# Turning h before its norm is known, and bringing the norm in late

## The chip, the cores and the metric

The kernel runs on one core of one Trainium2 chip. The metric is the device time of one execution in microseconds. Three runs of the kernel before took 1638.55, 1638.58 and 1638.84 us, median 1638.58.

## The reference, cut to what matters

One residual block over 512 tokens of width 1024. Its last third is the part that the change touches:

```
h   = h + merged @ w_out                       # 512 x 1024
hn  = h * rsqrt(mean(h*h) + 1e-6) * g_ffn      # one factor per token, one per channel
qry = hn @ w_peer_q                            # 1024 -> 2048: 8 heads x 2 halves x 128
s1, s2 = qry halves @ keys                     # 128 keys each
v1, i1 = top16(s1);  v2, i2 = top16(s2)
best   = top16 of the 16 x 16 sums v1 + v2     # per head and token
gates  = softmax(best)
out    = h + sum over 16384 experts of gate * gelu(u . hn) * v
```

The top lists do not change when all scores of a token are multiplied by one positive number. The softmax and the products `u . hn` do.

## The kernel before, in words

All products of full width run on TensorE in pieces that give nearly f32 accuracy. An operand is split into a high part (f32 rounded to TensorE's fp32r) and a low part (what is left), and three matmuls are made for each pair of blocks: high x high, high x low and low x high (`PARTS`). The weights come in 512 KB items, one after the other, through four raw buffers. For each item ScalarE makes the high part (`high_w`, line 1196) and GpSimd the low part (`low_ws`, line 435; VectorE takes a few, line 1515), into two buffers that alternate. An item of a projection is 24 matmuls of 128x512 on TensorE.

The order of the work on each engine is written out by hand: each engine has one instruction stream (blocks `@block.tensor`, `.scalar`, `.vector`, `.gpsimd`, `.sync`), and the streams meet at counting semaphores. SyncE issues all DMAs in its own order.

The stretch that the change touches runs like this:

- The output projection (items 77 to 84, lines 700 and 976) fills PSUM banks 0 to 3 with the left half of h, then banks 4 to 7 with the right half. VectorE adds x (`add_x`, line 1812), and ScalarE sums the squares (`square_h`, line 1373) and takes roots (line 1388).
- VectorE takes the reciprocals and multiplies h by them (`norm_h`, lines 1818 and 1821, result `h_scaled`). TensorE turns the 32 blocks of it (`turn_block`, line 656), 16 in each half of the width.
- ScalarE reads the turned blocks out of PSUM times g_ffn into the high part of `hT_r` (line 1396); VectorE makes the low part (line 1845) and then `x_two`, which is low x 128 + high (line 1851).
- The query projection has 16 items, number 85 to 100. The first (`first_item`, lines 670, 674, 678) goes along with the arriving blocks of `hT_r`, the others are plain (`t_item`, line 687). After item 1, and from then on after every second one, TensorE makes key scores (`key_scores`, line 1023, order in `SCORES_AFTER`), two groups each time, 16 groups in all. ScalarE copies the query out (`query`, line 1412), makes the high part of the item after the next, and then copies the scores out (`score_copy`, line 1401). There are two score buffers: the copy of group g waits until VectorE has finished the lists of group g - 2 (`at_least(act, score_used, g - 1)`).
- VectorE makes the top-16 lists of a group (`first_lists` and `top16`, lines 1862 to 1872).
- The up stage multiplies 128 tiles of u with the normed h (`up`, line 1061, 16 matmuls a tile): the first of the two operands is the high part of `hT_r`, the second is `x_two`. ScalarE makes the high part of each tile (`high_u`, line 1407), GpSimd the low part of the first 56 (line 474). ScalarE's stream at the join of the two stages is: query 15, copy of scores 14, `high_u(1)`, copy of scores 15, `high_u(2)`, then gelu 0 (line 1426) and so on.
- During the first 56 tiles VectorE makes the candidate sums, the second lists and the gates (lines 1884 to 1927), and TensorE turns each of four results between tiles 20, 33, 45, 52 and the next (`turn_lists`, line 656).

Of the kernel before, what the change touches and what calls it, by code (L numbers as in the profile page):

```python
# [24 lines left out]
F32 = mybir.dt.float32  # L25
# [3 lines left out]
ALU = mybir.AluOpType  # L29
# [3 lines left out]
P = 128  # L33
T = 512
# [71 lines left out]
SCORES_AFTER = {1: (0,), 3: (1, 2), 5: (3, 4), 7: (5, 6), 9: (7, 8), 11: (9, 10), 13: (11, 12), 14: (13,), 15: (14,)}  # L106
EXP_AFTER, TURN_AFTER = (10, 20, 31, 44), (20, 33, 45, 52)
# [12 lines left out]
def build(nc, A, out, gates_dram, pre_dram, acts_dram):  # L120
    ctx = ExitStack()
    with ctx:
# [34 lines left out]
        def carve_r(name, at, size):  # L157

            return carve(name, at, size, F32R)
# [45 lines left out]
        hT_r = carve_r("hT_r", 4096, 8192)  # L205
        x_two = carve_r("x_two", 34816, 4096)
        h_scaled = carve("h_scaled", 22528, 4096)
        junk = carve("junk", 43008, 1024)
# [34 lines left out]
        hs3 = h_scaled.rearrange("p (t d) -> p t d", d=D)  # L243
# [78 lines left out]
        def block_bank(k):  # L322
# [5 lines left out]
        max_out, max_in, if_in, f_row = sem("max_out"), sem("max_in"), sem("if_in"), sem("f_row")  # L328
# [7 lines left out]
        act_step, dve_step, pool_step = sem("act_step"), sem("dve_step"), sem("pool_step")  # L336
# [3 lines left out]
        h_half, h_biased = sem("h_half"), sem("h_biased")  # L340
# [7 lines left out]
        q_scaled, conv_done, silu_done, sig_o = sem("q_scaled"), sem("conv_done"), sem("silu_done"), sem("sig_o")  # L348
# [14 lines left out]
        h_rooted, h_normed, hT_done, hT_hi, hT_out = (  # L363
            sem("h_rooted"), sem("h_normed"), sem("hT_done"), sem("hT_hi"), sem("hT_out"))
# [38 lines left out]
        def _(pool):  # L403
# [74 lines left out]
        def _(sp):  # L478
# [30 lines left out]
            sp.dma_start(acts_dram[0, 0:4, :], r_max).then_inc(max_out, 16)  # L509
            loaded = I_KV - 1  # L510
            for m in range(24):
                while loaded <= gate_at(m) + 4:
                    load_item(loaded, loaded % 4)
                    loaded += 1
                if m == 1:
                    sp.wait_ge(max_out, 16)
                    sp.dma_start(r_all, acts_dram[0, 0:4, :].rearrange("h t -> (h t)").partition_broadcast(P)
                                 ).then_inc(max_in, 16)
# [28 lines left out]
            load_items(I_PQ + 4, ITEMS, len(DVE_LOW))  # L547
# [106 lines left out]
        def _(pe):  # L654
# [307 lines left out]

            for b in range(2):
                pe.wait_ge(br_used, 20 + 4 * b)
                for j in range(4):
                    n = I_OUT + 4 * b + j
                    if n < I_PQ - 2:
                        n_item(n, n % 2, j, 4 * b, gr4, TT, landed=m_lo if b == 0 else None)

# [22 lines left out]
            def turn_block(t, k):  # L992

                ins = turn(block_bank(k)[:, t * P:(t + 1) * P], hs3[:, t, k * P:(k + 1) * P])
                if t == TT - 1:
                    ins.then_inc(hT_done, 1)

            def turn_h(t, half):

                pe.wait_ge(h_normed, 2 * t + half + 1)  # L1000
                for k in range(4 * half, min(4 * half + 4, KD - 1)):
                    if t == 0 and k >= 3:
                        pe.wait_ge(h_out, TT + k - 2)
                    turn_block(t, k)

            def last_h():
                for t in range(TT):
                    turn_block(t, KD - 1)

            turn_h(0, 0)  # L1010
            turn_h(1, 0)
            turn_h(0, 1)
            turn_h(1, 1)
            for t in range(2, TT):
                turn_h(t, 0)
                turn_h(t, 1)
# [11 lines left out]
            for n in range(4):  # L1028
                if n:
                    t_item(I_PQ + n, (I_PQ + n) % 2, n, hr4)  # L1030
                else:
                    first_item(I_PQ, hr4, hT_hi, hT_out, last_h)
# [20 lines left out]
            def up(n, s, first=0, last=16):  # L1053


                for i in range(first, last):
                    k, w = i // 2, i % 2
                    if i == 0:
                        wait_low_u(pe, n)
                        at_least(pe, gelu_done, n - 1)  # L1060
                    ins = pe.matmul(bank(s % 2), u2[s][:, w, k * P:(k + 1) * P], x2[:, k, :] if w else hr4[:, 0, k, :],  # L1061
                                    start=i == 0, stop=i == 15, skip_group_check=True)
                if last == 16:
                    ins.then_inc(u_done, 1)
# [83 lines left out]
        def _(act):  # L1148
# [226 lines left out]

            for n in range(I_OUT + 2, I_PQ):
                high_w(n, n % 4)
                if n == I_OUT + 6:
                    for t in range(TT - 1):
                        link(square_h(0, t))  # L1380
                    square_h(0, TT - 1).then_inc(h_half, 1)

                    link(act.activation(roots[:, 60:61], eps_col[:, :], ACT.Sqrt))
            act.wait_ge(h_biased, 1)
            for t in range(TT):
                c_ = slice(S_H + t, S_H + t + 1)
                link(square_h(1, t))
                act.activation(roots[:, c_], sums[:, c_], ACT.Sqrt, bias=sums[:, S_H + 8 + t:S_H + 9 + t],
                               scale=1.0 / D).then_inc(h_rooted, 1)
                if t == 1:  # L1390
                    high_w(I_PQ, I_PQ % 4)
            high_w(I_PQ + 1, (I_PQ + 1) % 4)
            for k in range(KD):
                act.wait_ge(hT_done, k + 1)
                g_ = cols[:, C_FFN + k:C_FFN + k + 1]
                act.activation(hr4[:, 0, k, :], block_bank(k), ACT.Copy, scale=g_).then_inc(hT_hi, 1)
# [12 lines left out]
            def query(n):  # L1409
# [7 lines left out]
                for g in SCORES_AFTER.get(n, ()):  # L1417
                    score_copy(g, g)

# [14 lines left out]
            def gate_exp(t):  # L1434
                act.wait_ge(cand_top, t + 1)
                act.activation(lists[t % 2].gate, lists[t % 2].gate, ACT.Exp).then_inc(cand_exp, 1)
# [61 lines left out]
        def _(dve):  # L1498
# [25 lines left out]
            dve.tensor_scalar(qg_scaled[:, :], cols[:, C_QG:C_QG + 1], HD_SCALE, None, ALU.mult).then_inc(q_scaled, 1)  # L1524
# [139 lines left out]
            def decay(h):  # L1664

                if h == 0:
                    dve.wait_ge(max_in, 16)
                    dve.wait_ge(cols_out, 1)
# [145 lines left out]
            def norm_h(t):  # L1814

                c_ = slice(S_H + t, S_H + t + 1)
                dve.wait_ge(h_rooted, t + 1)
                link(dve.reciprocal(rstd[:, c_], roots[:, c_]))
                for b in range(2):
                    half = slice(b * BANK, (b + 1) * BANK)  # L1820
                    dve.tensor_scalar(hs3[:, t, half], h3[:, t, half], rstd[:, c_], None, ALU.mult).then_inc(h_normed, 1)

            dve.wait_ge(item_done, I_OUT + 4)
            for t in range(TT):
                add_x(0, t)
            dve.wait_ge(h_half, 1)
            dve.tensor_scalar(sums[:, S_H + 8:S_H + 12], sums[:, S_H + 4:S_H + 8], 1.0 / D, EPS, ALU.mult,
                              ALU.add).then_inc(h_biased, 1)
            low_w(I_PQ - 1)
            for t in range(TT):  # L1830
# [5 lines left out]
                if t == 1:  # L1836
                    norm_h(0)
                    norm_h(1)
            norm_h(2)
            norm_h(3)  # L1840

            for k in range(KD):
                g_ = cols[:, C_FFN + k:C_FFN + k + 1]
                dve.wait_ge(hT_hi, k + 1)
                dve.scalar_tensor_tensor(out=hr4[:, 1, k, :], in0=block_bank(k), scalar=g_, in1=hr4[:, 0, k, :].bitcast(F32),
                                         op0=ALU.mult, op1=ALU.subtract).then_inc(hT_out, 1)


            for k in range(KD):
                dve.wait_ge(hT_out, k + 1)  # L1850
                dve.scalar_tensor_tensor(out=x2[:, k, :], in0=hr4[:, 1, k, :].bitcast(F32), scalar=SPREAD,
                                         in1=hr4[:, 0, k, :].bitcast(F32), op0=ALU.mult,
                                         op1=ALU.add).then_inc(x2_made, 1)


# [249 lines left out]
```

## Time and profile before

| | |
|---|---|
| median of three runs | 1638.58 us |
| the profiled execution | 1638.45 us, span 1636.7 us |
| TensorE, busy share of the span | 100%, granted clock 1.0 of full speed |
| VectorE, ScalarE, GpSimd | 66%, 46%, 24% |
| DMA | 210 GB/s mean |

The span is the time from the first to the last instruction; the profiled execution took 1.75 us more than it. The times in rows are counted from the start of the span. A busy time of TensorE counts each matmul to its modelled end, which overlaps the next one; what a matmul costs in a row of many is the distance of their starts.

### The profile page before, as it was taken

To read this page: it belongs to the slowest core of one execution; us is meant where nothing else is said; L and a number is where in the kernel's file an instruction comes from. 1 tells how busy PE (TensorE), PEld (TensorE's weight loads), DVE (VectorE), ACT (ScalarE), POOL (GpSimd) and SP (SyncE) were. 2 spreads that over 40 slices of the span, in tenths; PEclk is the share of its full clock that TensorE was granted. 3 is DMA by queue.
4 is the path that set the end of the run, shared out by engine and by line. 5 is a ranking of instruction groups with operands and counts; after the bars stand their busy time and mean duration, and the time that the engine had idled before them with its cause. 6 is when DMAs were issued, how large, how long until landed. Compare 5 with 4: busy or idle time off the path is not lost.

```text
span 1636.7 us, 23665 instructions
## 1 busy us (share of the span) xinstructions
PE 1629.7 (100%) x8216; PEld 1350.7 (83%) x8216; DVE 1087.0 (66%) x1889; ACT 755.4 (46%) x941; POOL 395.8 (24%) x179
## 2 busy tenths in 40 slices
PE   9999999999999999999999999999999999999999
PEld 7888878788788888888888888888888888888887
DVE  4027554357483688999989999934466666666665
ACT  5242247644543424444545555545444444444442
POOL 3434323243253445787740000000000000000000
PEclk9999999999999999999999999999999999999999
DMA  5223353222543331666668888898698888888884
GB/s 198 99 93 100 103 180 97 96 78 88 208 167 103 103 127 55 220 217 217 215 206 296 315 300 310 295 321 295 242 317 287 284 293 288 295 292 283 285 290 159
DMA packets 165972, 344.42 MB, mean 210 GB/s; under 512 B 13068, under 2 KB 78604, under 8 KB 163600
## 3 DMA queue, kind: packets, MB, share of 16 engines
q1 hardware_dynamic: 165904, 343.53, 61.9%
q8 instruction: 41, 0.67, 0.2%
q14 instruction: 27, 0.22, 0.0%
HBM read 267.97 MB, written 75.51 MB: 210 GB/s over the span
## 4 chain that ended last, share of the span: by engine, by line
PE 92%; issue 4%; POOL 2%; ACT 1%; DVE 0%; POOLq 0%; ACTq 0%
PE ps L1070 28%; PE ps L1061 27%; PE ps L687 15%; PE ps L700 9%; PE ps L1099 4%; PE ps L955 3%; POOL w_r L435 1%; PE ps L827 1%; PE ps L1023 1%; PE ps L656 1%; POOL u_r L474 1%; PE ps L976 1%; PE ps L811 1%; PE ps L837 0%; POOL work L425 0%
## 5 line engine op out<-in xcount | busy, mean ns | idle before, releaser
L1070 PE MATMUL ps<-v_r,w_pairs 128*128 128x512 f32 x2036 | 461.7, 389 | 0.0
L1070 PEld LDWEIGHTS ps<-v_r,w_pairs 128*128 128x128 f32 x2036 | 382.3, 188 | 79.2
L1061 PE MATMUL ps<-hT_r,u_r 128*128 128x512 f32 x1024 | 400.8, 391 | 0.1
L1061 PE MATMUL ps<-x_two,u_r 128*128 128x512 f32 x1024 | 398.7, 389 | 0.0
L435 POOL TENSOR_TENSOR w_r<-w_raw,w_r 128x1024 fp32r<-128x1024 f32 x88 | 224.1, 2549 | 382.2 <-ACT w_r L1196 380.0
L2011 DVE TENSOR_TENSOR v_r<-vraw,v_r 128x1024 fp32r<-128x1024 f32 x128 | 156.8, 1225 | 150.4 <-ACT v_r L1479 150.4
L1479 ACT ACTIVATE v_r<-vraw 128x1024 fp32r<-128x1024 f32 x128 | 135.7, 1060 | 253.7 <-PE ps L1070 249.0
L1061 PEld LDWEIGHTS ps<-hT_r,u_r 128*128 128x128 f32 x1024 | 192.3, 188 | 40.4 <-POOL u_r L474 0.5
L1061 PEld LDWEIGHTS ps<-x_two,u_r 128*128 128x128 f32 x1024 | 192.3, 188 | 39.4
L687 PE MATMUL ps<-xT_r,w_r 128*128 128x512 f32 x936 | 218.8, 392 | 0.0
L687 PEld LDWEIGHTS ps<-xT_r,w_r 128*128 128x128 f32 x936 | 174.0, 188 | 36.9 <-issue 1.2
L1196 ACT ACTIVATE w_r<-w_raw 128x1024 fp32r<-128x1024 f32 x100 | 105.2, 1055 | 181.9 <-PE ps L700 79.3
L1426 ACT ACTIVATE act_stage<-ps 128x512 f32<-128x512 f32 x128 | 76.5, 598 | 225.9 <-PE ps L1061 225.8
L474 POOL TENSOR_TENSOR u_r<-uraw,u_r 128x1024 fp32r<-128x1024 f32 x56 | 159.7, 2861 | 48.1 <-ACT u_r L1407 48.0
L1407 ACT ACTIVATE u_r<-uraw 128x1024 fp32r<-128x1024 f32 x128 | 134.9, 1054 | 13.8 <-DMA uraw<-in_u 10.9
L1973 DVE TENSOR_TENSOR u_r<-uraw,u_r 128x1024 fp32r<-128x1024 f32 x72 | 87.6, 1223 | 63.3 <-ACT u_r L1407 63.2
L2007 DVE TENSOR_TENSOR w_f<-act_in,g_in 128x512 f32<-128x512 f32 x128 | 87.5, 684 | 6.8 <-issue 6.0
L2014 DVE SCALAR_TENSOR_TENSOR w_pairs<-w_pairs,w_f 128x512 fp32r<-128x512 f32 x128 | 87.5, 684 | 0.0
L700 PE MATMUL ps<-w_r,xT_r 128*128 128x512 f32 x384 | 87.3, 389 | 0.0
L700 PEld LDWEIGHTS ps<-w_r,xT_r 128*128 128x128 f32 x384 | 72.0, 188 | 15.1 <-POOL w_r L435 0.2
L687 PE MATMUL ps<-hT_r,w_r 128*128 128x512 f32 x360 | 83.9, 391 | 0.0
L1481 ACT ACTIVATE w_pairs<-w_f 128x512 fp32r<-128x512 f32 x128 | 78.6, 614 | 3.7 <-DVE w_f L2007 3.7
(268 smaller groups left out, 1713.0 us busy)
## 6 DMA issues: line engine op xcount, KB each, us to landing
uraw<-in_u SPq DMA_DIRECT2D x128, 512.0 KB, 5.0
vraw<-in_v SPq DMA_DIRECT2D x128, 512.0 KB, 5.4
w_raw<-in_w SPq DMA_DIRECT2D x101, 512.0 KB, 3.6
acts_out<-act_stage SPq DMA_DIRECT2D x128, 256.0 KB, 2.3
gates<-stage SPq DMA_DIRECT2D x16, 2048.0 KB, 7.4
g_in<-gates SPq DMA_DIRECT2D x64, 512.0 KB, 6.5
act_in<-acts_out SPq DMA_DIRECT2D x128, 256.0 KB, 5.3
gates_pre<-pre_stage SPq DMA_DIRECT2D x24, 256.0 KB, 2.3
```

The lines of the kernel that those rows point to most:

```text
L435: pool.tensor_tensor(wr4[:, n % 2, 1, :], raw3[:, n % 4, :], wr4[:, n % 2, 0, :].bitcast(F32), ALU.subtract).then_inc(w_lo_ready, 1)
L474: pool.tensor_tensor(u2[n % 4][:, 1, :], u_raw[n % 4], u2[n % 4][:, 0, :].bitcast(F32), ALU.subtract).then_inc(u_lo, 1)
L687: ins = pe.matmul(bank(b), wr4[:, s, ww, k * P:(k + 1) * P], act[:, wa, k, :], start=k == 0 and ww + wa == 0, stop=k == KD - 1 and ww == 1)
L700: ins = pe.matmul(bank(b0 + t), act[:, wa, 2 * j + k, t * P:(t + 1) * P], wr4[:, s, ww, k * BANK:(k + 1) * BANK], start=j == 0 and k == 0 ...
L1061: ins = pe.matmul(bank(s % 2), u2[s][:, w, k * P:(k + 1) * P], x2[:, k, :] if w else hr4[:, 0, k, :], start=i == 0, stop=i == 15, skip_gro ...
L1070: ins = pe.matmul(bank(2 * q + h), w2[:, s, w, q * P:(q + 1) * P], v2[s][:, w, h * BANK:(h + 1) * BANK], start=start and w == 0, stop=stop ...
L1196: act.activation(wr4[:, q % 2, 0, :], raw3[:, q, :], ACT.Copy).then_inc(w_hi_ready, 1)
L1407: act.activation(u2[s][:, 0, :], u_raw[s], ACT.Copy, scale=KEEP).then_inc(u_hi, 1)
L1479: act.activation(v2[s][:, 0, :], vr[:, s, :], ACT.Copy, scale=KEEP).then_inc(v_hi, 1)
L1973: dve.tensor_tensor(u2[s][:, 1, :], u_raw[s], u2[s][:, 0, :].bitcast(F32), ALU.subtract).then_inc(u_lo_dve, 1)
L2007: dve.tensor_tensor(wf[:, s % 2, :].rearrange("p (b t) -> p b t", t=BLK), ai3[:, s, :].rearrange("p (b t) -> p b t", t=BLK), g4[:, par, :, ...
L2011: dve.tensor_tensor(v2[s][:, 1, :], vr[:, s, :], v2[s][:, 0, :].bitcast(F32), ALU.subtract).then_inc(v_lo, 1)
```

## The change

Five things are moved or added.

1. h is turned without its factor. The 16 blocks of the left half are turned after the first item of the right half of the output projection, the 16 of the right half in pieces between the last matmuls of that projection and the first of the query projection. Their high and low parts are made from the unnormed h (times g_ffn), 4 blocks early, 4 late. `norm_h` and its 8 multiplications go, and so does `x_two` from this place.
2. The first query item starts with the four early blocks. GpSimd no longer waits for `h_normed`.
3. The sums of squares are added, rooted and inverted once for all four token blocks: ScalarE's last two squares come in `query(0)`, the root in `query(1)`; VectorE's add and reciprocal stand ahead of the first list. The four columns of factors are turned on TensorE after query item 2, copied out by ScalarE, written to DRAM, and read back spread over all partitions (`rstd_h`, 128 x 512); SyncE waits for this between weight loads.
4. The softmax takes the factor as the scale of its exponential.
5. The up operands are made late. VectorE makes, in pairs of blocks, high + low (two adds) and that times 128 times `rstd_h` (two multiplications) after lists 1, 2, 4 and 5 (`widen`). ScalarE makes the high part `hn_r` from it after query items 6 and 10 (`high_hn`). VectorE makes `x_two` from both after lists 3 and 7 (`second_of`), four blocks each time.

```diff
+HN_AFTER = {6: (0, 1, 2, 3), 10: (4, 5, 6, 7)}
+WIDE_AFTER, X2_AFTER = {1: 0, 2: 2, 4: 4, 5: 6}, {3: (0, 2), 7: (4, 6)}
...
-            low_ws(I_PQ, 1)
-            pool.wait_ge(h_normed, 2 * TT)
-            low_ws(I_PQ + 1, ITEMS - I_PQ - 1)
+            low_ws(I_PQ, ITEMS - I_PQ)
...
-            load_items(I_PQ + 4, ITEMS, len(DVE_LOW))
+            for n in range(I_PQ + 4, I_PQ + 8):
+                load_item(n, n % 4)
+            sp.wait_ge(h_row, 1)
+            sp.dma_start(acts_dram[2, 0, :].rearrange("(t p) -> t p", p=P), rstd_q[0:TT, :]).then_inc(row_out, 16)
+            sp.wait_ge(row_out, 32)
+            sp.dma_start(rstd_h, acts_dram[2, 0, :].partition_broadcast(P)).then_inc(row_in, 16)
+            load_items(I_PQ + 8, ITEMS, len(DVE_LOW))
...
+                    if n == I_OUT + 4:
+                        pe.wait_ge(h_out, TT)
+                        for k in range(4):
+                            for t in range(TT):
+                                turn_block(t, k)
...
+            pe.wait_ge(hT_out, 4)
+            turn_second(0)
+            turn_second(1)
             out_part(3, 2).then_inc(out_tile, 1)
             out_part(3, 3).then_inc(item_done, 1)
...
+            pe.wait_ge(w_hi_ready, I_PQ)
+            for k in range(4):
+                query_part(k, 0, 0)
+                query_part(k, 0, 1)
+            turn_second(2)
+            turn_second(3)
+            take_item(I_PQ)
+            for k in range(4):
+                query_part(k, 1, 0)
+            for k in range(4, KD + 1):
+                if k < KD:
+                    pe.wait_ge(hT_hi, k + 1)
+                    query_part(k, 0, 0)
+                    query_part(k, 1, 0)
+                if k > 4:
+                    pe.wait_ge(hT_out, k)
+                    ins = query_part(k - 1, 0, 1)
...
+                if n == 2:
+                    pe.wait_ge(h_rstd, 1)
+                    turn(bank(6)[0:TT, 0:P], rstd[:, S_H:S_H + TT]).then_inc(h_rstd, 1)
...
+            def high_hn(k):
+                act.wait_ge(h_widened, k + 1)
+                act.activation(hn3[:, k, :], hw3[:, k % 4, :], ACT.Copy, scale=1.0 / SPREAD).then_inc(hn_made, 1)
...
+            def widen(k):
+                dve.wait_ge(hT_out, k + 2)
+                at_least(dve, h_widened, k)
+                at_least(dve, x2_made, k - 2)
+                for i in (k, k + 1):
+                    ins = dve.tensor_tensor(hs3[:, i % 2, :], hr4[:, 0, i, :].bitcast(F32), hr4[:, 1, i, :].bitcast(F32),
+                                            ALU.add)
+                link(ins)
+                for i in (k, k + 1):
+                    dve.scalar_tensor_tensor(out=hw3[:, i % 4, :], in0=hs3[:, i % 2, :], scalar=SPREAD, in1=rstd_h,
+                                             op0=ALU.mult, op1=ALU.mult).then_inc(h_widened, 1)
+            def second_of(k):
+                for i in (k, k + 1):
+                    dve.wait_ge(hn_made, i + 1)
+                    dve.scalar_tensor_tensor(out=x2[:, i, :], in0=hn3[:, i, :].bitcast(F32), scalar=1.0 - SPREAD,
+                                             in1=hw3[:, i % 4, :], op0=ALU.mult, op1=ALU.add).then_inc(x2_made, 1)
...
             for g in range(2 * PH):
                 first_lists(g)
+                if g == 1:
+                    dve.wait_ge(row_in, 32)
+                if g in WIDE_AFTER:
+                    widen(WIDE_AFTER[g])
+                for k in X2_AFTER.get(g, ()):
+                    second_of(k)
```

Most buffers of this stage get new places in SBUF.

## Rows read from the trace of the kernel before

**Rows 1.** The page: busy time of engines, and shares of the last chain.

```profile
PE 1629.7 (100%) x8216; PEld 1350.7 (83%) x8216; DVE 1087.0 (66%) x1889; ACT 755.4 (46%) x941; POOL 395.8 (24%) x179
...
PE 92%; issue 4%; POOL 2%; ACT 1%; DVE 0%; POOLq 0%; ACTq 0%
```

**Rows 2.** Waits of TensorE: engine, line, releaser, total us, times, longest.

```profile
PE ps L656 <- POOL iota_top L418: 2.8, 1, 2.8
...
PE ps L656 <- DVE h_scaled L1821: 0.2, 1, 0.2
```

**Rows 3.** Timeline of TensorE: start us, length us, engine, line, operation, count.

```profile
525.11 11.12 PE L976 MATMUL ps<-w_r,merged_r 128*128 128x512 f32 x48
536.07 2.52 PE L656 MATMUL ps<-ident,h_scaled 128*128 128x128 f32 x21
...
546.07 5.60 PE L687 MATMUL ps<-hT_r,w_r 128*128 128x512 f32 x24
...
614.11 1.95 PE L1023 MATMUL ps<-keysT,qryT 128*128 128x128 f32 x16
615.81 11.14 PE L687 MATMUL ps<-hT_r,w_r 128*128 128x512 f32 x48
...
649.50 0.39 PE L1061 MATMUL ps<-hT_r,u_r 128*128 128x512 f32 x1
```

**Rows 4.** Timeline of VectorE through the query projection; in brackets the idle before.

```profile
545.18 4.89 DVE L1851 SCALAR_TENSOR_TENSOR x_two<-hT_r 128x512 fp32r<-128x512 f32 x8
...
565.65 0.88 DVE L1862 MAX8 top_lists<-scores 128x8 f32<-128x128 f32 x4 [6.70 <-ACT scores L1401]
...
570.74 0.85 DVE L1862 MAX8 top_lists<-scores 128x8 f32<-128x128 f32 x4
...
578.33 0.88 DVE L1862 MAX8 top_lists<-scores 128x8 f32<-128x128 f32 x4 [2.43 <-ACT scores L1401]
...
644.29 0.85 DVE L1862 MAX8 top_lists<-scores 128x8 f32<-128x128 f32 x4
```

**Rows 5.** VectorE's wait for scores, summed.

```profile
DVE top_lists L1862 <- ACT scores L1401: 22.6, 7, 6.7
```

**Rows 6.** Timeline of ScalarE: the h blocks, and the join of the stages.

```profile
539.18 4.73 ACT L1396 ACTIVATE hT_r<-ps,cols 128x512 fp32r<-128x512 f32 x8 [0.19 <-PE ps L656]
...
641.46 0.60 ACT L1401 ACTIVATE scores<-ps 128x512 f32<-128x512 f32 x1 [0.29 <-PE ps L1023]
...
644.46 0.60 ACT L1401 ACTIVATE scores<-ps 128x512 f32<-128x512 f32 x1 [1.46 <-DVE top_lists L1872]
644.96 1.06 ACT L1407 ACTIVATE u_r<-uraw 128x1024 fp32r<-128x1024 f32 x1
```

**Rows 7.** Timeline of GpSimd: low parts of weight items, and of u tile 2.

```profile
547.89 4.43 POOL L435 TENSOR_TENSOR w_r<-w_raw,w_r 128x1024 fp32r<-128x1024 f32 x1 [6.12 <-ACT w_r L1196]
...
577.88 2.40 POOL L435 TENSOR_TENSOR w_r<-w_raw,w_r 128x1024 fp32r<-128x1024 f32 x1 [3.04 <-ACT w_r L1196]
...
603.25 2.40 POOL L435 TENSOR_TENSOR w_r<-w_raw,w_r 128x1024 fp32r<-128x1024 f32 x1 [3.03 <-ACT w_r L1196]
...
646.09 2.40 POOL L474 TENSOR_TENSOR u_r<-uraw,u_r 128x1024 fp32r<-128x1024 f32 x1 [0.62 <-ACT u_r L1407]
```

**Rows 8.** Timeline of VectorE in the branch mix.

```profile
454.59 1.29 DVE L1785 TENSOR_TENSOR gate_s<-ps,gate_s 128x512 f32<-128x512 f32 x2 [4.15 <-PE ps L955]
455.79 3.48 DVE L1792 TENSOR_TENSOR mergedT<-mergedT,gate_s 128x512 f32<-128x512 f32 x2
```

**Rows 9.** Timeline of GpSimd at the same place.

```profile
455.78 2.94 POOL L435 TENSOR_TENSOR w_r<-w_raw,w_r 128x1024 fp32r<-128x1024 f32 x1 [3.04 <-ACT w_r L1196]
```

**Rows 10.** DMA issues: KB each, us from issue to landing.

```profile
r_all<-acts_out SPq DMA_DIRECT2D x1, 1024.0 KB, 6.6
```

**Rows 11.** VectorE and TensorE at the first result of the second lists.

```profile
716.02 0.29 DVE L1927 TENSOR_TENSOR top_small<-top_small 128x128 f32<-128x128 f32 x1
...
718.42 0.49 PE L656 MATMUL ps<-ident,top_small 128*128 128x128 f32 x3
```

More of the change, by code:

```diff
@@ L204, in build @@
         h_res = carve("h_res", 0, 4096)
-        hT_r = carve_r("hT_r", 4096, 8192)
+        hT_r = carve_r("hT_r", 38912, 8192)
+        hn_r = carve_r("hn_r", 4096, 4096)
         x_two = carve_r("x_two", 34816, 4096)
-        h_scaled = carve("h_scaled", 22528, 4096)
-        junk = carve("junk", 43008, 1024)
+        rstd_h = carve("rstd_h", 34304, T)
+        rstd_q = carve("rstd_q", 47104, P)
+        junk = carve("junk", 47104, 1024)
+        h_sum = carve("h_sum", 48128, 2 * T)
+        h_wide = carve("h_wide", 49152, 4 * T)
         u_raw = [carve(f"uraw{s}", at, 1024) for s, at in enumerate((12288, 13312, 22528, 23552))]
@@ L961, in _, with h_bank, turn_block, turn_second @@
                 branch(b)
+            def h_bank(k):
+                return bank(k if k < 4 else k - 3)
+            def turn_block(t, k):
+                ins = turn(h_bank(k)[:, t * P:(t + 1) * P], h3[:, t, k * P:(k + 1) * P])
+                if t == TT - 1:
+                    ins.then_inc(hT_done, 1)
+            def turn_second(t):
+                pe.wait_ge(h_out, TT + t + 1)
+                for k in range(4, KD):
+                    turn_block(t, k)
             for b in range(2):
@@ L988, in _, with query_part @@
             out_part(2, 3).then_inc(item_done, 1)
+            pe.wait_ge(hT_out, 4)
+            turn_second(0)
+            turn_second(1)
             out_part(3, 2).then_inc(out_tile, 1)
             out_part(3, 3).then_inc(item_done, 1)
[L992 to L1016, printed above, removed]
+            def query_part(k, ww, wa):
+                return pe.matmul(bank(0), wr4[:, I_PQ % 2, ww, k * P:(k + 1) * P], hr4[:, wa, k, :],
+                                 start=k + ww + wa == 0, stop=k + wa == KD)
+            pe.wait_ge(w_hi_ready, I_PQ)
[15 more added lines that the diff above has]
+                    ins = query_part(k - 1, 0, 1)
+            ins.then_inc(item_done, 1)
             def key_scores(g, s):
@@ L1060, in up @@
                         at_least(pe, gelu_done, n - 1)
-                    ins = pe.matmul(bank(s % 2), u2[s][:, w, k * P:(k + 1) * P], x2[:, k, :] if w else hr4[:, 0, k, :],
+                    ins = pe.matmul(bank(s % 2), u2[s][:, w, k * P:(k + 1) * P], x2[:, k, :] if w else hn3[:, k, :],
                                     start=i == 0, stop=i == 15, skip_group_check=True)
@@ L1418, in query @@
                     score_copy(g, g)
+                if n == 0:
+                    link(square_h(1, 2))
+                    square_h(1, 3).then_inc(h_squared, 1)
+                if n == 1:
+                    act.wait_ge(h_squared, 2)
+                    act.activation(roots[:, S_H:S_H + TT], sums[:, S_H:S_H + TT], ACT.Sqrt, bias=eps_col[:, :],
+                                   scale=1.0 / D).then_inc(h_rooted, 1)
+                if n == 2:
+                    act.wait_ge(h_rstd, 2)
+                    act.activation(rstd_q[0:TT, :], bank(6)[0:TT, 0:P], ACT.Copy).then_inc(h_row, 1)
+                for k in HN_AFTER.get(n, ()):
+                    high_hn(k)
             def gelu(n, s):
@@ L1435, in gate_exp @@
                 act.wait_ge(cand_top, t + 1)
-                act.activation(lists[t % 2].gate, lists[t % 2].gate, ACT.Exp).then_inc(cand_exp, 1)
+                act.activation(lists[t % 2].gate, lists[t % 2].gate, ACT.Exp,
+                               scale=rstd[:, S_H + t:S_H + t + 1]).then_inc(cand_exp, 1)
             high_u(2, 2)
@@ L1812, in add_x, with low_h @@
                 dve.tensor_tensor(h3[:, t, c_], bank(4 * b + t), xa3[:, t, c_], ALU.add).then_inc(h_out, 1)
[L1814 to L1821, printed above, removed]
+            def low_h(k):
+                dve.wait_ge(hT_hi, k + 1)
+                dve.scalar_tensor_tensor(out=hr4[:, 1, k, :], in0=bank(k if k < 4 else k - 3),
+                                         scalar=cols[:, C_FFN + k:C_FFN + k + 1], in1=hr4[:, 0, k, :].bitcast(F32),
+                                         op0=ALU.mult, op1=ALU.subtract).then_inc(hT_out, 1)
             dve.wait_ge(item_done, I_OUT + 4)
@@ L1825, in _ @@
                 add_x(0, t)
-            dve.wait_ge(h_half, 1)
-            dve.tensor_scalar(sums[:, S_H + 8:S_H + 12], sums[:, S_H + 4:S_H + 8], 1.0 / D, EPS, ALU.mult,
-                              ALU.add).then_inc(h_biased, 1)
+            for k in range(4):
+                low_h(k)
             low_w(I_PQ - 1)
@@ L1835, in _ @@
                 add_x(1, t)
[L1836 to L1853, printed above, removed]
+            for k in range(4, KD):
+                low_h(k)
+            dve.wait_ge(h_squared, 1)
+            dve.tensor_tensor(sums[:, S_H:S_H + TT], sums[:, S_H:S_H + TT], sums[:, S_H + TT:S_H + 2 * TT],
+                              ALU.add).then_inc(h_squared, 1)
+            dve.wait_ge(h_rooted, 1)
+            dve.reciprocal(rstd[:, S_H:S_H + TT], roots[:, S_H:S_H + TT]).then_inc(h_rstd, 1)
+            def widen(k):
[14 more added lines that the diff above has]
+                                             in1=hw3[:, i % 4, :], op0=ALU.mult, op1=ALU.add).then_inc(x2_made, 1)
             def top16(vals, idx, width, src, src2):
```

56 lines of the change are left out of this document (28 added, 28 removed).

## The prediction, made before the change was run

> **What bounds the kernel now.** I read the page's busy times and its chain first. TensorE is busy 100% of the span and makes up 92% of the last chain [rows 1]. So the kernel is as long as TensorE's stream, and a change can win only what TensorE idles and lose only where it is made to wait. Next the waits of TensorE: apart from 2.8 us at the start the longest is 0.2 us [rows 2]. The timeline at the change shows a little more than that list does. TensorE's turns begin at 536.07 and query item 1 begins at 546.07: 10.00 us [rows 3]. In these stand 32 turns and 24 matmuls. A matmul costs (536.07 - 525.11) / 48 = 0.228 us; a 128x128 operation in f32 costs (615.81 - 614.11) / 16 = 0.106 us [rows 3], which I take for a turn. That makes 3.4 + 5.5 = 8.9 us, so 1.1 us are lost there. This is all that the change can win in this place.
>
> Last I read VectorE, ScalarE and GpSimd through the query projection, because the change moves work there. One group of lists takes 5.09 us (565.65 to 570.74), and two groups come every 12.68 us (565.65 to 578.33), so VectorE idles 2.5 us in each period [rows 4]. Its waits for scores sum to 22.6 us in 7 times [rows 5], the two longest ahead of lists 0 and 1.
>
> **The change part by part.**
>
> *The turns.* The same 32 turns and 24 matmuls run, in pieces. Let 0 be the end of out_part(3,1). TensorE then makes 12 matmuls (to 2.7), 8 turns (3.6), 12 matmuls (6.3), 8 matmuls of the query (8.1), 8 turns (9.0), 4 matmuls (9.9), and the rest as blocks arrive. VectorE's adds of x, with one input in PSUM, take some 0.65 us (1.29 for two, [rows 8]) and follow each finished tile, so the last turns find h ready. ScalarE makes the four late blocks at 0.59 us each (8 in 4.73, [rows 6]): from about 8.9 they are ready at 9.5, 10.1, 10.7, 11.3, wanted at 9.9, 10.4, 11.0, 11.7. VectorE's low parts follow closely, the last with some 0.1 us of wait. GpSimd's low part of item 85, 2.4 us from about 4.1, is wanted at 9.0. There are two more changes between turns and matmuls than before, and each loses something; I leave 0.2 of the 1.1 us lost. Saved: 0.9 us, between 0 and 1.1. The turn of the four columns of factors adds one small operation, 0.1 us.
>
> *VectorE in the query projection.* It loses `norm_h` and the early `x_two`, but those stood ahead of list 0, which waited for scores anyway; nothing comes of that. The 8 old operations ran from 545.18, and list 1 waited 6.70 us [rows 4]. Item 0's root and reciprocal now stand ahead of list 0: ScalarE reaches the root right after the copy of scores 0, so list 0 begins some 0.5 us later, and the wait before list 1 takes that up. After list 1 the change adds 16 operations for `widen` and 8 for `second_of`, each over 512 elements of 128 partitions with two inputs in SBUF. The nearest row is the old `x_two`, same shape and kind, 8 in 4.89, so 0.611 each [rows 4]: 24 x 0.611 = 14.7, and with the four waits on itself between adds and multiplications 15.0 us. Upper bound: 0.68 each, its length standing alone, 16.3; the lower bound is 14.7 itself, no row of this shape being shorter.
>
> What takes it up: from 570.74 the lists 2 to 13 need 12 x 5.09 = 61.1 us and would end at 631.8. They end at 644.29 [rows 4], so 12.5 us of idle are there. 15.0 - 12.5 = 2.5 us are not covered. List 13 is the one that matters, as below.
>
> *GpSimd against VectorE.* Two adds of 128x512 with both inputs in SBUF took 3.48 us, where two with one input in PSUM took 1.29 [rows 8]. In that time GpSimd ran its subtraction from SBUF, 2.94 us in place of 2.40 [rows 9, 7]. So either waits until the other is through. The same shows at 547.89, where GpSimd's subtraction took 4.43 beside the old `x_two` [rows 7]. The lists don't do this: GpSimd's 2.40 at 577.88 and 603.25 lie beside them or beside idle. Laid out in the times of before:
> - `widen(0)` 570.7 to 573.3, GpSimd (from 572.5) waits 0.8, no harm; list 2 to 578.4.
> - `widen(2)` finds GpSimd at work 577.88 to 580.28 [rows 7]: 1.9 us of wait; done 582.8; list 3 to 587.9; `second_of` to 590.3; list 4 to 595.4; `widen(4)` to 597.9; list 5 to 603.0.
> - `widen(6)`: the adds 603.0 to 604.2, GpSimd, ready at 603.25, gets in between adds and multiplications, another 2.3 us; done 607.8. Lists 6, 7 to 618.0; `second_of` to 620.5; lists 8 to 13 to 651.0.
>
> That is 6.7 us later than 644.29, 4.2 of them from GpSimd. The bounds of this term are 0 and one hold of 2.2 us for each of the six blocks, 13; two holds is what the layout gives.
>
> *Who waits for VectorE.* ScalarE copies scores 15 only when list 13 is done (it already waited 1.46 us for this, [rows 6]). Behind that copy in its stream stands `high_u(2)`, then GpSimd's low part of tile 2 and TensorE's up(2). Before: list 13 done 644.29, copy 644.46, high part 644.96, low part 646.09 to 648.49 [rows 6, 7]; up(2) began at 649.50, 32 matmuls behind the first of the stage [rows 3]. So there is 1.0 us of slack, and TensorE is 6.7 - 1.0 = 5.7 us late at up(2). Part of it shows earlier: the copy of scores 8 waits for list 6 (612.9) and holds query 10 (due 608.9) and the high part of item 12, whose low part is then ready at 617.3 for an item due at 615.81 [rows 3], 1.5 us; up(1) waits as well, behind the copy of scores 14. These lie inside the 5.7, not on top: the chain through VectorE has no gap after list 1. Nothing gives it back later, TensorE being full to the end.
>
> *The rest.* SyncE's wait: ScalarE copies the row of factors at about 559.7; it is written, then read back to all partitions. The nearest row is the 1024 KB spread of another row, 6.6 us [rows 10]. Twice that is 572.9, 2.2 too late for `widen(0)`; with a quarter of the bytes I take half of it, in time. Queued behind it on SyncE is the load of item 93, whose high part is made after query item 6, some 10 us later than that. ScalarE's eight `high_hn` (0.59 each) fall into waits for TensorE or behind a late query, inside the same chain. The exponential with a scale, the unused semaphores and the new buffer places: nothing. Second lists: the first result was ready at 716.31, wanted at 718.42 [rows 11]. VectorE is 6.7 late there, TensorE 5.7, so 1.1 of 2.1 us remain.
>
> **Sum.** -0.9 (turns) + 0.1 (factors) + 5.7 (VectorE's lateness at up(2)) = +4.9; I round the holds down a little, 4.8. On the profiled execution's 1638.45 (0.13 below the median of the runs): 1643.2 us.
>
> **A rule on these holds.** The Trainium skill (SBUF — State Buffer, "SBUF: two separate sides") says that the one which starts first keeps the shared ports for its whole instruction, and then the other goes. In [rows 7] at 547.89 the subtraction waited 2.03 us, so past the ends of three VectorE operations of 0.611, where that rule lets it in after the first; in [rows 8] it did get in after one.
>
> **The rivals.**
> - *GpSimd gets in at every end of an operation.* For it: [rows 8, 9]; against it: 547.89 in [rows 7]. Then it also gets in within `widen(0)` (after which `widen(2)` meets no GpSimd), `widen(6)` and the second `second_of`: three holds of 2.3 in place of 4.2 in all, and waits on ends add up to 2.8 more: 1646.0. (So it would be by the Trainium skill's rule above.) A spread of factors that lands 2.2 late ends near there too.
> - *No holds.* GpSimd's subtractions fall beside the lists, or it always waits itself. For it: GpSimd waited at 547.89, and `widen(6)` misses it by 0.2 us. Then 2.5 - 1.0 - 0.8: +0.7, 1639.2.
> - *Not slower: the lateness dies in the slack.* Place: list 13. If the 24 operations take no more than 13.5 us together (0.56 each) and meet no GpSimd, up(2) is on time, and only the turns count: 1637.7. Against it: 0.611 in [rows 4].
> - *The turns win nothing* (ScalarE or VectorE late with the four blocks): 0.9 more on any of these; it is inside the ranges.
>
> **How the numbers follow.** Forecast 45% (own range 1641.4 to 1645.4), every-end rival 18%, no holds 24%, lateness dies 10%, something worse 3% (a third hold in the second lists, 1648). A measurement of this kernel tells 0.2%, 3.3 us, from no change: slower is above 1641.9. Slower: 38 of the 45, the 18 and 2 of the 3: 58%. Faster needs 3.3 us where 1.1 are lost: 3%, for what no row prices. Same: 39%. The range 1638.4 to 1646.6 leaves out the "dies" case, the low edge of no holds and the high edges: 20%.
>
> **What would show it.** TensorE from the last out_part to item 1 with less than 0.4 us lost. In VectorE's timeline `widen(2)` and `widen(6)` with a wait of about 2 us, list 13 ending 5 to 7 us later against TensorE's items, and no waits for scores after list 1. ScalarE's copies of scores 8, 10, 14 and 15 waiting for lists, TensorE waiting for low parts at item 12, up(1) and up(2). It is wrong if list 13 still waits for scores, or if up(2) begins earlier than 650.

## The result, and the profile after

The changed kernel took 1644.35 us (median of 7 runs, 1644.26 to 1644.76), the kernel before 1638.79 (7 runs beside it): a ratio of 1.0034, interval 1.0023 to 1.0046. It is slower by 5.6 us, and the interval does not reach 1. The forecast was 1643.2, 4.8 above the profiled execution of the kernel before. The rows below answer to those of before.

The page of the changed kernel: busy times, and the chain that ended last.

```profile
PE 1632.2 (99%) x8217; PEld 1352.3 (82%) x8217; DVE 1098.0 (67%) x1894; ACT 759.6 (46%) x947; POOL 400.2 (24%) x179
...
PE 83%; DVE 10%; issue 4%; POOL 2%; ACT 0%; POOLq 0%; ACTq 0%
```

In [rows 1] VectorE had 0% of that chain. Now it has 10%: through the query projection the lists, not the matmuls, lead to the end. The waits of TensorE (columns as in [rows 2]):

```profile
PE ps L668 <- POOL iota_top L426: 2.8, 1, 2.8
PE ps L1096 <- POOL u_r L480: 2.0, 1, 2.0
PE ps L699 <- ACT qryT L1453: 1.7, 1, 1.7
PE ps L668 <- DVE top_small L1986: 0.6, 1, 0.6
```

The first was there before. The other three are new, and name up(1), item 12 and the first turn of list results. A wait in this list starts at the modelled end of the last matmul, some 0.16 us after the next one could have begun (0.39 long, 0.228 apart), so each costs about that much more than it says. The timeline of TensorE, against [rows 3, 11]:

```profile
545.54 5.63 PE L699 MATMUL ps<-hT_r,w_r 128*128 128x512 f32 x24
...
617.28 11.16 PE L699 MATMUL ps<-hT_r,w_r 128*128 128x512 f32 x48 [1.67 <-ACT qryT L1453]
...
649.55 0.50 PE L1096 MATMUL ps<-hn_r,u_r 128*128 128x512 f32 x1 [2.02 <-POOL u_r L480]
...
654.93 0.39 PE L1096 MATMUL ps<-hn_r,u_r 128*128 128x512 f32 x1
...
724.65 0.55 PE L668 MATMUL ps<-ident,top_small 128*128 128x128 f32 x3 [0.62 <-DVE top_small L1986]
```

Distances between the same instructions tell where the 6.3 us between the two profiled spans went. VectorE's first add of x stood at 514.50 before and stands at 514.87 now, so 0.4 came earlier, in a part that the change doesn't touch (the profiled execution is also 0.4 above the median of its kernel). From that add to query item 1 it was 31.57 us and is 30.67: the turns won 0.9. From item 1 (546.07, now 545.54) to up(2) (649.50, now 654.93) it was 103.43 and is 109.39: 6.0 lost. From up(2) to the first turn of list results it was 68.92 and is 69.72: 0.8 lost. Behind it nothing moves (918.3 us to the end before, 918.4 now).

VectorE, against [rows 4]:

```profile
565.21 0.87 DVE L1921 MAX8 top_lists<-scores 128x8 f32<-128x128 f32 x4 [6.52 <-ACT scores L1442]
...
570.30 1.27 DVE L1901 TENSOR_TENSOR h_sum<-hT_r 128x512 f32<-128x512 f32 x2
571.62 3.49 DVE L1905 SCALAR_TENSOR_TENSOR h_wide<-h_sum,rstd_h 128x512 f32<-128x512 f32 x2
...
604.12 3.37 DVE L1905 SCALAR_TENSOR_TENSOR h_wide<-h_sum,rstd_h 128x512 f32<-128x512 f32 x2
...
617.56 2.48 DVE L1912 SCALAR_TENSOR_TENSOR x_two<-hn_r,h_wide 128x512 fp32r<-128x512 f32 x4
...
650.41 0.85 DVE L1921 MAX8 top_lists<-scores 128x8 f32<-128x128 f32 x4
...
722.27 2.32 DVE L1986 TENSOR_TENSOR top_small<-top_small 128x128 f32<-128x128 f32 x1
```

No list after list 1 waits for scores, and `widen(0)` starts right behind list 1, so the row of factors was there in time. Where a list ends the next one starts, so the line at 650.41 is the end of list 13. From the end of list 1 to the end of list 13 (650.41) it is 80.1 us where it was 73.6: 6.6 more. Counted from item 1, which is how TensorE meets it, list 13 ends at 104.87 in place of 98.22: 6.65 later. GpSimd at the same places, against [rows 7]:

```profile
572.01 2.55 POOL L443 TENSOR_TENSOR w_r<-w_raw,w_r 128x1024 fp32r<-128x1024 f32 x1 [4.84 <-ACT w_r L1231]
...
602.80 3.53 POOL L443 TENSOR_TENSOR w_r<-w_raw,w_r 128x1024 fp32r<-128x1024 f32 x1 [2.73 <-ACT w_r L1231]
...
618.28 4.01 POOL L443 TENSOR_TENSOR w_r<-w_raw,w_r 128x1024 fp32r<-128x1024 f32 x1 [1.15 <-ACT w_r L1231]
...
647.14 2.35 POOL L480 TENSOR_TENSOR u_r<-uraw,u_r 128x1024 fp32r<-128x1024 f32 x1 [7.25 <-ACT u_r L1448]
652.21 2.39 POOL L480 TENSOR_TENSOR u_r<-uraw,u_r 128x1024 fp32r<-128x1024 f32 x1 [2.72 <-ACT u_r L1448]
```

Two multiplications of `widen` take 1.3 us where GpSimd is quiet, 3.49 and 3.37 where it is not: 2.2 + 2.1 = 4.3 us of holds. The two multiplications one by one, of `widen(0)` and of `widen(6)` (shortest, median and longest in ns, then the starts):

```profile
L1905 DVE SCALAR_TENSOR_TENSOR h_wide<-h_sum,rstd_h x2: 691/1786/2882, 571.6 to 572.2; 128x512 f32<-128x512 f32 x2
...
L1905 DVE SCALAR_TENSOR_TENSOR h_wide<-h_sum,rstd_h x2: 676/1721/2766, 604.1 to 606.8; 128x512 f32<-128x512 f32 x2
```

In `widen(0)` the second one is held: it starts at 572.2, GpSimd, which asked at 572.01, is at work until 574.56, and the multiplication ends at 575.1. In `widen(6)` it is the first: GpSimd asked at 602.80, just as the two adds began, got in only behind both of them, and ran until 606.3. ScalarE, first its wait for lists over the whole span, then its timeline at scores 8 and at the join ([rows 6]):

```profile
ACT scores L1442 <- DVE top_lists L1931: 36.8, 8, 9.1
```

```profile
612.67 0.60 ACT L1442 ACTIVATE scores<-ps 128x512 f32<-128x512 f32 x1 [9.07 <-DVE top_lists L1931]
...
650.59 0.60 ACT L1442 ACTIVATE scores<-ps 128x512 f32<-128x512 f32 x1 [3.52 <-DVE top_lists L1931]
651.09 1.05 ACT L1448 ACTIVATE u_r<-uraw 128x1024 fp32r<-128x1024 f32 x1
```

The chain at the join is the one of before, later: list 13 at 650.41, copy 650.59, high part 651.09, low part 652.21 to 654.60, up(2) at 654.93. The last step has a second cause. up(1) began 0.06 us after its low part was done (647.14 + 2.35, then 649.55), up(2) 0.33 us after its own. TensorE was still busy with up(1) until then, because half of up(1) ran at half clock (last section). So some 0.3 us of the lateness at up(2) are the clock's.

### The profile page after: what moved, and what is told of

It reads as the page before. It is cut to its first block, busy times and chain, and to the rows that moved or that the text cites. A ratio compares the mean times of both kernels' runs of the same rounds, so it can differ in the third digit from the quotient of the medians.

```text
span 1643.0 us, 23676 instructions
## 1 busy us (share of the span) xinstructions
PE 1632.2 (99%) x8217; PEld 1352.3 (82%) x8217; DVE 1098.0 (67%) x1894; ACT 759.6 (46%) x947; POOL 400.2 (24%) x179
## 4 chain that ended last, share of the span: by engine, by line
PE 83%; DVE 10%; issue 4%; POOL 2%; ACT 0%; POOLq 0%; ACTq 0%
PE ps L1105 28%; PE ps L1096 23%; PE ps L699 11%; PE ps L712 9%; PE ps L1134 4%; PE ps L967 3%; POOL w_r L443 1%; PE ps L839 1%; DVE top_lists L1931 1%; DVE top_lists L1924 1%; PE ps L668 1%; DVE top_in L1925 1%; DVE top_lists L1928 1%; POOL u_r L480 1%; DVE top_lists L1921 1%
## 5 line engine op out<-in xcount | busy, mean ns | idle before, releaser
L1096 PE MATMUL ps<-hn_r,u_r 128*128 128x512 f32 x1024 | 401.8, 392 | 2.1 <-POOL u_r L480 2.0
L1096 PEld LDWEIGHTS ps<-hn_r,u_r 128*128 128x128 f32 x1024 | 192.8, 188 | 43.0 <-POOL u_r L480 2.9
L480 POOL TENSOR_TENSOR u_r<-uraw,u_r 128x1024 fp32r<-128x1024 f32 x56 | 163.1, 2922 | 49.5 <-ACT u_r L1448 49.3
```

What stands on the lines that cost most here:

```text
L480: pool.tensor_tensor(u2[n % 4][:, 1, :], u_raw[n % 4], u2[n % 4][:, 0, :].bitcast(F32), ALU.subtract).then_inc(u_lo, 1)
```

## The experiments

The kernel before ran beside each experiment on its chip: median 1638.66 us (27 runs) beside e1 to e4, 1638.70 (21 runs) beside e5 to e7. It was 1638.79 beside the changed kernel, so a difference between medians of different sets is good to some 0.1 us. In the diffs, `...` stands for lines left out.

**e1: the turns alone.** The 24 late operations are out, so the up operands lack the token's factor.

```diff
             def high_hn(k):
 
-                act.wait_ge(h_widened, k + 1)
-                act.activation(hn3[:, k, :], hw3[:, k % 4, :], ACT.Copy, scale=1.0 / SPREAD).then_inc(hn_made, 1)
+                act.activation(hn3[:, k, :], hr4[:, 0, k, :].bitcast(F32), ACT.Copy).then_inc(hn_made, 1)
...
             for k in range(4, KD):
                 low_h(k)
+            for k in range(KD):
+                dve.wait_ge(hT_out, k + 1)
+                dve.scalar_tensor_tensor(out=x2[:, k, :], in0=hr4[:, 1, k, :].bitcast(F32), scalar=SPREAD,
+                                         in1=hr4[:, 0, k, :].bitcast(F32), op0=ALU.mult,
+                                         op1=ALU.add).then_inc(x2_made, 1)
...
-                if g in WIDE_AFTER:
-                    widen(WIDE_AFTER[g])
-                for k in X2_AFTER.get(g, ()):
-                    second_of(k)
```

> The changed kernel with the 24 late VectorE operations taken out: x_two is made ahead of list 0 from the unnormed h, as in the kernel before, and ScalarE only copies the high part. The up operands lack the token's factor; everything else (turns in pieces, late root, factor row, scale in the softmax) stays. My theory (the turns win 0.9 us, the lists' lateness loses 5.7 or more): the lists wait for scores again from list 3 on, TensorE never waits at item 12, up(1), up(2) or the first turn of list results, 1637.7 to 1638.2. Rival (the turns in pieces, the row of factors on SyncE or the moved buffers cost time themselves): 1639.5 to 1644.

Measured 1638.45 (11 runs, 1638.26 to 1639.15), ratio 0.9999, 0.9990 to 1.0008: 0.25 us above the range that I expected, and not to be told from the kernel before. TensorE's stretch to item 1 is 0.9 us shorter here too (514.75 to 545.38, 30.63). The missing part is seen in the timelines of GpSimd and of TensorE at item 2:

```profile
547.20 4.84 POOL L443 TENSOR_TENSOR w_r<-w_raw,w_r 128x1024 fp32r<-128x1024 f32 x1 [4.42 <-ACT w_r L1232]
```

```profile
552.10 5.74 PE L699 MATMUL ps<-hT_r,w_r 128*128 128x512 f32 x24 [0.19 <-POOL w_r L443]
```

Eight VectorE operations in a row hold GpSimd's low part of item 2 as they did before, but TensorE now comes earlier and meets it: item 2 begins 0.4 us later than in the changed kernel (6.72 behind item 1, there 551.82, 6.28). So the turns' gain is real, and all of the loss hangs on the 24 operations: without them TensorE loses only these 0.4 us and 0.2 more between item 2 and up(2) (97.29 in place of 97.12), where the factors' turn stands.

**e2: one input of each of the 24 from PSUM.** Same count, shape and place; the up operands lack what the replaced input holds.

```diff
-   ... hr4[:, 0, i, :].bitcast(F32), hr4[:, 1, i, :].bitcast(F32), ALU.add)
+   ... hr4[:, 0, i, :].bitcast(F32), bank(7), ALU.add)
...
-   ... scalar=SPREAD, in1=rstd_h,
+   ... scalar=SPREAD, in1=bank(7),
...
-   ... in1=hw3[:, i % 4, :], op0=ALU.mult
+   ... in1=bank(7), op0=ALU.mult
```

> The changed kernel with one input of each of the 24 operations read from PSUM bank 7 in place of SBUF, so that they have one SBUF input; the values of the up operands are wrong by this. Same count, shape and place. Theory (two holds by GpSimd, 4.2 us, are part of the loss): the multiplications after lists 1 and 5 take 1.3 us for two in place of 3.4, list 13 ends some 4 us earlier than in the changed kernel, up(2) starts at most 2 us late, 1640.0 to 1641.0. Rival (the holds don't matter, ScalarE's order or something else paces TensorE): over 1643.5.

Measured 1640.00 (11 runs, 1639.75 to 1640.32), ratio 1.0008, 0.9999 to 1.0017: 4.35 us below the changed kernel's median. The multiplications after lists 1 and 5 in its timeline:

```profile
571.55 1.28 DVE L1905 SCALAR_TENSOR_TENSOR h_wide<-h_sum,ps 128x512 f32<-128x512 f32 x2
...
601.78 1.28 DVE L1905 SCALAR_TENSOR_TENSOR h_wide<-h_sum,ps 128x512 f32<-128x512 f32 x2
```

The length of an operation is the same and the holds are gone. Counted from item 1, list 13 ends at 100.48, 4.4 us earlier than in the changed kernel. About three quarters of the loss are GpSimd's holds; what stays is the uncovered work, 2.3 us at list 13. TensorE still waits 1.0 us at up(2) and 0.6 at the first turn of list results.

**e3: the order at the join.** ScalarE makes the high parts of tiles 1 and 2 before it waits for list 12, and copies scores 15 after gelu 0.

```diff
                 for g in SCORES_AFTER.get(n, ()):
-                    score_copy(g, g)
+                    if g < 14:
+                        score_copy(g, g)
...
             high_u(1, 1)
-            score_copy(15, 15)
+            high_u(2, 2)
+            score_copy(14, 14)
...
-            high_u(2, 2)
             for n in range(N_TOP):
                 gelu(n, n % 4)
                 if n < N_TOP - 1:
                     high_u(n + 3, (n + 3) % 4)
+                if n == 0:
+                    score_copy(15, 15)
```

> The changed kernel with ScalarE's order at the join changed: high_u(1) and high_u(2) ahead of the copy of scores 14, gelu 0 and high_u(3) ahead of the copy of scores 15. Theory A (TensorE's loss is the lists' lateness, which has a second consumer just behind): TensorE no longer waits at up(1) and up(2), but waits 4 us or more at the first turn of list results instead; 1642.5 to 1644.5. Theory B (the order of ScalarE's stream at the join is the cause): 1639.5 to 1641.

Measured 1645.77 (5 runs, 1645.28 to 1646.20), ratio 1.0042, 1.0028 to 1.0056. Theory B falls. Theory A holds for the place and the size of the wait, but the time is 1.3 us above its range. The new and the kept wait of TensorE, and two windows (columns: busy us of PE, PEld, DVE, ACT, POOL, then the granted clock, DMA share, GB/s):

```profile
PE ps L668 <- DVE top_small L1989: 4.2, 1, 4.2
...
PE ps L699 <- ACT qryT L1453: 1.6, 1, 1.6
```

```profile
719.00:723.90 4.90, 0.75 (x4) 0.29 (x2) 4.83 (x5) 2.83 (x3) 4.59 (x2) 0.85 0.65 237
723.90:728.50 4.60, 4.55 (x13) 3.69 (x14) 4.53 (x7) 1.69 (x2) 0.00 (x0) 0.50 0.00 0
```

The wait moved from the join to the turn, as foretold; the one at item 12 stayed. The rest is the granted clock: it fell during the 4.2 us without work (0.85 in the first window) and is 0.50 of full speed, 1.2 GHz, in the next 4.6 us. Eleven matmuls there run at half speed, 0.427 us apart in place of 0.228, which costs 2.2 us.

**e4: the 8 adds early.** They move into the idle ahead of list 1.

```diff
+                if g == 0:
+                    dve.wait_ge(hT_out, KD)
+                    for i in range(KD):
+                        ins = dve.tensor_tensor(h_sums[:, i * T:(i + 1) * T], hr4[:, 0, i, :].bitcast(F32),
+                                                hr4[:, 1, i, :].bitcast(F32), ALU.add)
+                    link(ins)
...
-                for i in (k, k + 1):
-                    ins = dve.tensor_tensor(hs3[:, i % 2, :], hr4[:, 0, i, :].bitcast(F32), hr4[:, 1, i, :].bitcast(F32),
-                                            ALU.add)
-                link(ins)
```

> The changed kernel with the 8 adds high + low moved between list 0 and list 1, where VectorE idles 6.5 us; the sums lie where x_two comes later. 16 operations of 0.61 us (9.8 us) stay behind list 1, against 12.5 us of idle. Theory (the loss is what the idle behind list 1 doesn't cover): list 13 ends on time or at most 2 us late, 1637.7 to 1639.5. Rival (ScalarE or GpSimd meet the blocks anyway, or the high parts after query items 6 and 10 hold VectorE): 1640 to 1643.

Measured 1640.27 (11 runs, 1640.12 to 1640.90), ratio 1.0010, 1.0001 to 1.0019. It gives 4.1 of the 5.6 us back and is still 0.8 above my range, inside the rival's, which named the reasons. GpSimd, VectorE and TensorE:

```profile
559.43 8.90 POOL L444 TENSOR_TENSOR w_r<-w_raw,w_r 128x1024 fp32r<-128x1024 f32 x2 [3.95 <-ACT w_r L1232]
```

```profile
586.62 4.29 DVE L1909 SCALAR_TENSOR_TENSOR x_two<-hn_r,h_wide 128x512 fp32r<-128x512 f32 x4 [2.10 <-ACT hn_r L1438]
```

```profile
566.12 11.13 PE L700 MATMUL ps<-hT_r,w_r 128*128 128x512 f32 x48 [0.97 <-POOL w_r L444]
```

The first row is two low parts. That of item 4, due to take 2.40, took 6.54 because it was held behind the 8 adds, and TensorE waited 1.0 for it. After list 3 VectorE now arrives before ScalarE has made the high parts: 2.1 us of wait, and 1.8 more in a hold.

**e5: the same, mended.**

```diff
-WIDE_AFTER, X2_AFTER = {1: 0, 2: 2, 4: 4, 5: 6}, {3: (0, 2), 7: (4, 6)}
-EXP_AFTER, TURN_AFTER = (10, 20, 31, 44), (20, 33, 45, 52)
+WIDE_AFTER, X2_AFTER = {1: 0, 2: 2, 5: 4, 6: 6}, {4: (0, 2), 8: (4, 6)}
+EXP_AFTER, TURN_AFTER = (10, 20, 31, 44), (21, 33, 45, 52)
...
+            sum_blocks(0)
...
+                if g == 0:
+                    sum_blocks(4)
```

Here `sum_blocks(k)` makes the four adds from block k on; the first call stands ahead of list 0, the second between list 0 and list 1.

> The version with early sums, mended where its trace showed waits: 4 of the 8 adds ahead of list 0 and 4 behind it (8 in one row held GpSimd's low part of item 4, and TensorE waited 1.0 us), the pairs of widen after lists 1, 2, 5, 6 and second_of after lists 4 and 8 (ScalarE's high parts were 2.1 us late for list 3), and the first turn of list results one tile later. Theory (all that TensorE lost were waits that VectorE's placing makes): no wait of TensorE over 0.3 us behind the query's first item, the turns' 0.9 us show, 1637.8 to 1638.5 where the kernel before has 1638.7. Rival (waits come back elsewhere, at item 2 or in the second lists): 1639 to 1641.

Measured 1637.89 (11 runs, 1637.67 to 1638.10), in the range expected; the kernel before beside it 1638.70 (21 runs, 1638.46 to 1639.09). The ratio is 0.9994, interval 0.9985 to 1.0003, so by the interval it can't be told from the kernel before, though no run of the one reaches into those of the other. It is 6.5 us below the changed kernel. All waits of TensorE that its trace lists:

```profile
PE ps L669 <- POOL iota_top L427: 2.8, 1, 2.8
PE ps L669 <- DVE xs L1576: 0.4, 1, 0.4
PE ps L683 <- ACT xT_r L1238: 0.3, 1, 0.3
PE ps L968 <- POOL w_r L444: 0.2, 1, 0.2
```

None is in the query projection or behind it. All four stand in the parts that the change leaves alone. Counted from item 1, list 13 ends at 98.30, on time (98.22 before). Three placings were mended at once, so this run shows that the waits were all of the loss, not what each mend is worth.

**e6: four more operations.** After list 8, four operations like `second_of`, results unused.

```diff
+                if g == 8:
+                    for i in range(4):
+                        dve.scalar_tensor_tensor(out=o_, in0=hn3[:, i, :], scalar=1.0 - SPREAD, in1=hw3[:, i % 4, :], ...)
```

> The changed kernel with four more VectorE operations of the kind of second_of after list 8, results unused: 2.4 us more. Theory (TensorE's loss is the lists' lateness, one for one): list 13 ends 2.4 us later, TensorE at up(2) as well, 1646.3 to 1647.3. Rival (part of the lateness has slack, or TensorE's loss comes from elsewhere): under 1645.5.

Measured 1646.85 (5 runs, 1646.78 to 1647.12), ratio 1.0050, 1.0036 to 1.0064: 2.5 us above the changed kernel for 2.4 us of work. Counted from item 1 its list 13 ends at 107.27 (104.87 in the changed kernel), 2.4 later, and up(2) starts 2.4 later as well. TensorE's wait at up(1) grew from 2.0 to 3.1, and a new one of 1.1 stands at the key scores, behind a query copy that waited for lists:

```profile
PE ps L1096 <- POOL u_r L480: 3.1, 1, 3.1
...
PE ps L1057 <- ACT qryT L1453: 1.1, 1, 1.1
```

**e7: the join of e3, and the consumers of the second lists put back.** The edit of e3, and this:

```diff
-EXP_AFTER, TURN_AFTER = (10, 20, 31, 44), (20, 33, 45, 52)
+EXP_AFTER, TURN_AFTER = (12, 22, 33, 46), (22, 34, 46, 53)
```

> The changed kernel with ScalarE's order at the join changed as in the run before, and the later consumers of the second lists put back as well: exponentials after tiles 12, 22, 33, 46 and turns after 22, 34, 46, 53. Theory (the lateness lies in the lists and is lost where the first consumer waits; given later consumers, only item 12's 1.7 us and some 2 us at the first gate groups are left): 1640.0 to 1642.5, no wait at up(1), up(2) or the turns. Rival (the lists' lateness comes back in full at the gate groups): 1643.5 to 1646.

Measured 1641.87 (11 runs, 1641.66 to 1642.40), ratio 1.0020, 1.0011 to 1.0029: 2.5 us below the changed kernel, 3.9 below e3. Its waits of TensorE behind the query's first item:

```profile
PE ps L699 <- ACT qryT L1453: 1.7, 1, 1.7
PE ps L1134 <- DVE onehots L2037: 1.2, 1, 1.2
PE ps L1096 <- POOL u_r L480: 0.5, 1, 0.5
```

The lateness of the lists costs what its consumers make it cost. With the consumers moved back it still shows in the last tiles of this stretch (0.5 us at 830.28) and at the first gate groups (1.2 us at 853.10): VectorE was busy 178.2 of the 180 us from 650 to 830, so it could not catch up.

## Why the prediction was right

The time alone would not have told the forecast (1643.2) from the rival "at every end" (1646.0): 1644.35 lies between them, 1.15 above the one and 1.65 below the other, and the range held both. What decides is the traces, term by term.

- **The turns: -0.9 forecast, -0.9 measured,** in the changed kernel and again in e1. All that TensorE lost at that place was 1.1 us, which had bounded the gain.
- **VectorE's uncovered work: 2.5 forecast, 2.3 measured** at list 13 in e2, which has no holds. Its time is 1.3 us above the kernel before. By the sum of the prediction it should be +0.7, plus 0.6 of the wait at the first turn of list results. e6 shows the exchange, 2.4 us of work for 2.5 us of time, and so that the idle behind list 1 is used up.
- **The holds: 4.2 forecast, 4.3 measured,** 4.35 in time by e2 (4.2 with each kernel set against the kernel before beside it). The count was right and one place wrong. I had put the first hold at `widen(2)`, with `widen(0)` making GpSimd wait at no cost. In the trace GpSimd got in between the two multiplications of `widen(0)`, and list 2 was so late that `widen(2)` met no GpSimd, as the rival "at every end" had it. The second, at `widen(6)`, came as laid out. That rival's third hold, in `second_of`, did not come: four in a row took 2.48 us, and GpSimd waited (4.01 in place of 2.40). So neither picture of who gets in is right everywhere. That the layout came to the right sum is partly luck: the hold in `widen(0)`, which it did not have, cost as much as the one in `widen(2)` that it took away.
- **The chain to up(2): 5.7 later forecast, 6.0 measured, with the factors' turn.** List 13 is 6.65 late (6.7 forecast), and the copy of scores 15, the high part and the low part follow as foretold. Less the 1.0 of slack that is 5.65; the other 0.3 are up(1)'s half clock, which the prediction had not priced. Item 12 (1.5 forecast, 1.7 measured) and up(1) lay inside it. At item 12 the prediction had the low part come last. It was done at 617.14, but the copy of query 11, behind four `high_hn` in ScalarE's stream, only at 617.26, and the wait is put down to that copy; the step differs, by 0.1 us. e3 shows that the copy's place in ScalarE's stream was not the cause, only the first place where the lateness was felt.
- **What I had not priced:** 0.8 us at the first turn of list results. I had left 1.1 of 2.1 us of slack there. The last operation of that result (722.27) took 2.32 us in place of the 0.29 of [rows 11]. GpSimd's subtraction ran from 722.06 to 724.45, so this is a hold, which I had given only as an unlikely extra. With it the sum of the steps is -0.9 + 6.0 + 0.8 = 5.9, against the 4.9 of the prediction; the medians are 5.6 apart.
- **The spread of factors:** taken as in time, at half of two transfers of 6.6 us. The read back was issued at 560.47 and landed 3.4 us later, 6.4 us ahead of `widen(0)`.
- **A reading that was wrong:** the longest wait of TensorE before, apart from the one at the start, is not 0.2 us. The trace also has one of 0.3 at 12.4 us. It lies far ahead of the change, and no term hangs on it.

The Trainium skill (SBUF — State Buffer, "SBUF: two separate sides") has the one that starts first keep the ports for its whole instruction. In `widen(0)` GpSimd got in at the first end and the next multiplication waited for its whole instruction, so that agrees. In `widen(6)` GpSimd waited past the end of the first add and got in behind the second; in `second_of` and the 8 adds of e4 it got in only at the end of the row. There the trace does not agree that the other goes at the first end: that it is let in after each instruction can't be counted on here.

It stays open what decides whether GpSimd gets in between two VectorE operations. Between two of a kind it got in at `widen(0)` and in [rows 8]. In `widen(6)` it got in where VectorE waits on itself, between adds and multiplications; the rows of 4 and 8 have no such wait within them, but neither has the pair of multiplications in `widen(0)`. No run changed only this.

## What to carry to other kernels

Before work is moved off a short gap of the busiest engine, count the idle of the engine that takes it, gap by gap, behind the last long wait: here 12.5 us were there for 15.0, the gap to be won was 1.1, and GpSimd's holds added 4.3. Then look where a late result is consumed first: moving that consumer alone (e3) moved the wait to the next one and made the kernel 1.4 us slower, and placing the work so that the lists were on time (e5) removed it. Operations that need no late factor, as the eight adds here, belong into the long idle ahead of it, in rows short enough that the engine sharing the ports still makes its own due time.

## What the runs showed of the hardware

Waits of TensorE of 2.0 us and of 4.2 us cost more than their length. Window of the changed kernel behind up(1)'s wait (columns as above):

```profile
649.60:654.00 4.40, 4.40 (x12) 3.45 (x13) 4.33 (x30) 3.38 (x5) 1.79 (x1) 0.61 0.00 0
```

TensorE's matmuls of up(0) ended at 647.5, up(1) began at 649.55, and from 650.6 to 653.8 its matmuls start 0.427 us apart, half speed. up(1) took 5.38 us in place of 3.63. Of the 1.75 us all but some 0.3 were hidden, since up(2) had to wait for its low part until 654.60 anyway; in e3, after a wait of 4.2 us, 2.2 us came on top. After the wait of 1.7 at item 12, and that of 1.0 at up(2) in e2, the granted clock stayed at 1.00. What decides between these cases no run here shows.
